# Heads' scores from high and low parts, softmax scaling on ScalarE and gate blocks of 384 columns in a decoder layer

## What is computed

```python
H_SB, H_MOBA, H_DSA, HEAD_DIM = 6, 5, 5, 64
def hybrid_mixer(h, w_in, b_gate, w_proj_sb, w_proj_moba, w_proj_dsa, w_o, slopes):
    proj = h @ w_in
    (q_sb, k_sb, v_sb, q_mb, k_mb, v_mb, q_ds, k_ds, v_ds,
     q_ix, k_ix, w_ix, gate_logits) = jnp.split(proj, _mixer_split_points(), axis=-1)
    o_sb = stick_breaking_attention(heads(q_sb), heads(k_sb), heads(v_sb))
    o_mb = moba_attention(heads(q_mb), heads(k_mb), heads(v_mb), slopes[0::2])
    o_ds = dsa_attention(heads(q_ds), heads(k_ds), heads(v_ds), q_ix..., k_ix, w_ix, slopes[1::2])
    g_sb, g_mb, g_ds = jnp.split(jax.nn.sigmoid(gate_logits + b_gate), N_BRANCH, axis=-1)
    merged = g_sb * (o_sb @ w_proj_sb) + g_mb * (o_mb @ w_proj_moba) + g_ds * (o_ds @ w_proj_dsa)
    return merged @ w_o
```

## Time and profile before

| | |
|---|---|
| median of 3 runs | 456.76 us (456.65 to 457.12) |
| the profiled execution | 456.9 us |
| its span, first to last instruction | 455.2 us |
| granted TensorE clock, mean | 0.996 |
| first projection units (0 to 9) | until about 56 us |
| units 10 to 50, with the heads | 56 to 213 us |
| merged heads and output projection | 213 to 261 us |
| SwiGLU | 261 to 455 us |

### The profile page before, as it was taken

How to read it: one execution, slowest core, us unless ns; L and a number is a source line. 1 busy time by engine, 2 the same in 40 slices (tenths; PEclk the granted TensorE clock), 3 DMA queues, 4 the chain that set the end, 5 groups by cost and what they waited for, 6 DMA issues and landing times.

```text
span 455.2 us, 7884 instructions
## 1 busy us (share of the span) xinstructions
PE 440.2 (97%) x2966; PEld 388.9 (85%) x2966; DVE 330.7 (73%) x587; ACT 243.6 (54%) x432; POOL 35.1 (8%) x76
## 2 busy tenths in 40 slices
PE   5999999999999999999999999999999999999994
PEld 3678998999999899999997899888888888888883
DVE  4625659887898887866995785896696687677655
ACT  4413885565777755587554676443534525425332
POOL 2000102100322231000000001000000000000000
PEclk9999999999999999999999999999999999999998
DMA  8999376797688558745559516998748658530002
GB/s 291 383 377 341 115 257 200 278 303 261 233 286 308 157 185 313 237 140 194 181 224 351 203 49 194 371 314 268 234 157 291 201 184 275 185 138 0 1 0 92
DMA packets 61634, 99.86 MB, mean 219 GB/s; under 512 B 3892, under 2 KB 44452, under 8 KB 61604
## 3 DMA queue, kind: packets, MB, share of 16 engines
q1 hardware_dynamic: 56480, 81.57, 52.8%
q0 software_dynamic: 4960, 17.84, 11.2%
q10 hardware_dynamic: 164, 0.05, 0.0%
HBM read 98.40 MB, written 1.05 MB: 218 GB/s over the span
## 4 chain that ended last, share of the span: by engine, by line
PE 91%; DVE 4%; issue 2%; ACT 2%; DMA 1%; SPq 0%; DVEq 0%; ACTq 0%
PE psum L1579 17%; PE psum L1982 16%; PE psum L1580 16%; PE psum L1581 16%; PE psum L1983 8%; PE psum L1641 3%; PE psum L1929 3%; PE psum L1595 2%; PE psum L1768 1%; DVE wlo L1113 1%; DMA xt<-in_x_dram 1%; PE psum L1703 1%; PE psum L1701 1%; PE psum L1630 1%; PE psum L1750 1%
## 5 line engine op out<-in xcount | busy, mean ns | idle before, releaser
L1982 PE MATMUL psum<-hcut,whi 128*128 128x512 f32 x320 | 111.5, 392 | 0.0
L1983 PE MATMUL psum<-hcut,wlo 128*128 128x256 f32 x320 | 89.5, 280 | 0.0
L1579 PE MATMUL psum<-hcut,whi 128*128 128x256 f32 x280 | 82.1, 293 | 0.3 <-DVE wlo L1113 0.3
L1580 PE MATMUL psum<-hcut,whi 128*128 128x256 f32 x280 | 79.1, 283 | 0.0
L1581 PE MATMUL psum<-hcut,wlo 128*128 128x256 f32 x280 | 79.1, 282 | 0.0
L1113 DVE TENSOR_TENSOR wlo<-raw,whi 128x768 fp32r<-128x768 f32 (+3 forms) x68 | 64.4, 972 | 15.6 <-ACT whi L749 15.0
L1982 PEld LDWEIGHTS psum<-hcut,whi 128*128 128x128 f32 x320 | 59.9, 187 | 13.2
L1983 PEld LDWEIGHTS psum<-hcut,wlo 128*128 128x128 f32 x320 | 60.4, 189 | 0.3
L749 ACT ACTIVATE whi<-raw 128x768 fp32r<-128x768 f32 (+3 forms) x68 | 55.6, 850 | 6.4 <-PE psum L1893 3.2
L1579 PEld LDWEIGHTS psum<-hcut,whi 128*128 128x128 f32 x280 | 53.4, 191 | 5.5 <-ACT qk L829 1.8
L1580 PEld LDWEIGHTS psum<-hcut,whi 128*128 128x128 f32 x280 | 53.5, 191 | 0.0
(11 more groups left out here) (252 smaller groups left out, 830.8 us busy)
## 6 DMA issues: line engine op xcount, KB each, us to landing
raw<-in_w_up_dram SPq DMA_DIRECT2D x22, 1024.0 KB, 7.5
xn<-in_w_ada_dram POOLq DMA_DIRECT2D x32, 512.0 KB, 4.9
raw<-in_w_in_dram SPq DMA_DIRECT2D x6, 2048.0 KB, 8.9
draw<-in_w_down_dram SPq DMA_DIRECT2D x11, 1024.0 KB, 5.0
ada<-in_w_ada_dram SPq DMA_DIRECT2D x16, 384.0 KB, 9.3
raw<-in_w_in_dram SPq DMA_DIRECT2D x3, 1536.0 KB, 8.9
raw<-in_w_o_dram SPq DMA_DIRECT2D x8, 512.0 KB, 4.5
raw<-in_w_in_dram SPq DMA_DIRECT2D x3, 1280.0 KB, 7.2
```

Source lines behind the costliest of these rows:

```text
L1579: pe.matmul(dst, a[0], b[0], start=first, stop=False)
L1580: pe.matmul(dst, a[0], b[1], start=False, stop=False)
L1982: pe.matmul(dst[:, :], wh, hcut[:, k, :, :].rearrange("p a s -> p (a s)"), start=k == 0, stop=False)
L1983: mm = pe.matmul(dst[:, S:2 * S], wl, hhi[:, k, :], start=False, stop=k == KC - 1)
```

## The change

Four things:

- **Parts for scores.** Of the 16 units with queries or keys of mb, sb and ds heads (`LOW_UNITS`) ScalarE writes the high part, in float32r, into `qk_hi`, and VectorE makes the low part (`take_low`), 20 instructions in all, into free columns of `whi` and `wlo` (`qk_low`). Scores are then `head_products`: three passes for each of the two column ranges, heads of a pair in turn. The indexer's logits stay float32.
- **New waits.** A new semaphore `unit_low`: TensorE's `unit(u)` waits for the low part of unit u-2 where it has one, since the bank is written again; the scores wait for theirs, and the first two logit pairs for those of units 5 to 9. In VectorE's order the low part of unit u-1 stands first in unit u.
- **Scaling.** The reciprocal stays on VectorE (`sum_inverse`), the two multiplications go to ScalarE, after its output copy of the same unit.
- **Blocks.** Gate blocks have 384 columns: 8 blocks of 3 units in place of 6 of 4. This leaves columns 3072 to 4095 of each `whi` and `wlo` free for the low parts. `PIECES_AT` follows: two, one and one piece over three units, and for the block after the last one three and one.

```diff
+GATE_COLS = 3 * P
+GATE_BLOCKS = 3 * D // GATE_COLS
-MIX_BLOCKS += [(O_GATE + BANK * i, BANK) for i in range(GATE_BLOCKS)]
+MIX_BLOCKS += [(O_GATE + GATE_COLS * i, GATE_COLS) for i in range(GATE_BLOCKS)]
...
+LOW_UNITS = [n for n, u in enumerate(UNITS) if u[1] in ("two heads", "last head") or u[1] == "features" and u[4] >= T_QMB]
...
+        def qk_low(tile):
+            i = LOW_SLOT[tile]
+            return (whi + wlo)[i // 4][:, KC * GATE_COLS + S * (i % 4):KC * GATE_COLS + S * (i % 4 + 1)]
...
+                elif u in LOW_UNITS:
+                    for tile, p0, s0, np, scale in qk_parts(u):
+                        ins = act.activation(qk_hi[p0:p0 + np, tile, :], src[s0:s0 + np, 0:S], ACT.Copy, scale=scale)
...
+                if u in NORM_AT and NORM_AT[u] in SOFT_NO:
+                    n = NORM_AT[u]
+                    act.wait_ge(sum_inverse, SOFT_NO[n] + 1)
+                    for t, (c0, c1) in enumerate(((0, P), (P, CAUSAL))):
+                        ins = act.activation(bufp[n % 2][:, c0:c1], bufp[n % 2][:, c0:c1], ACT.Copy, scale=ssum[:, n % 2, t:t + 1])
+                    ins.then_inc(p_ready, 1)
...
+            def take_low(u):
+
+                dve.wait_ge(unit_read, 2 * (u // 2) + 2 if u < FIRST_UNIT else u + 1)
+                src = unit_place(u)
+                for tile, p0, s0, np, scale in qk_parts(u):
+                    low, high = qk_low(tile)[p0:p0 + np, :], qk_hi[p0:p0 + np, tile, :].bitcast(F32)
+                    ins = dve.scalar_tensor_tensor(low, src[s0:s0 + np, 0:S], scale, high, ALU.mult, ALU.subtract)
+                ins.then_inc(unit_low, 1)
...
             for u in range(FIRST_UNIT, N_UNITS):
+                for m in [m for m in LOW_UNITS if m == u - 1 or u == FIRST_UNIT and m < u]:
+                    take_low(m)
...
-                    then(dve.reciprocal(ssum[:, n % 2, :], ssum[:, n % 2, :]))
-                    for t, (c0, c1) in enumerate(((0, P), (P, CAUSAL))):
-                        ins = dve.tensor_scalar(bufp[n % 2][:, c0:c1], bufp[n % 2][:, c0:c1], ssum[:, n % 2, t:t + 1], None, ALU.mult)
-                    ins.then_inc(p_ready, 1)
+                    dve.reciprocal(ssum[:, n % 2, :], ssum[:, n % 2, :]).then_inc(sum_inverse, 1)
...
                     pe.wait_ge(unit_read, u - 1)
+                    if u - 2 in LOW_UNITS:
+                        pe.wait_ge(unit_low, lows_until(u - 2))
...
+            def head_products(heads, cols, rows, fresh, done=None):
+
+                for i, (a, b) in enumerate(((0, 0), (0, 1), (1, 0))):
+                    for dst, left, right, p0 in heads:
+                        mm = pe.matmul(dst[:, cols], left[a][p0:p0 + HD, rows[0]], right[b][p0:p0 + HD, rows[1]], start=fresh and i == 0,
+                                       stop=i == 2, skip_group_check=True)
+                        if done is not None and i == 2:
+                            mm.then_inc(done, 1)
+
+            def query_major_cut(heads, done):
+
+                head_products(heads, slice(0, P), (slice(0, P), slice(0, P)), True)
+                head_products(heads, slice(P, CAUSAL), (slice(P, S), slice(0, S)), True, done)
```

More of the change, by code:

```diff
@@ L122, in mix_units @@
     for g in range(3 * D // P):
-        units.append((11 + g // 4, "gate", g % 4 * P, P, g))
+        units.append((11 + g * P // GATE_COLS, "gate", g * P % GATE_COLS, P, g))
     return units
@@ L129, with lows_until @@
 FIRST_GATE = N_UNITS - 3 * D // P
+LOW_UNITS = [n for n, u in enumerate(UNITS) if u[1] in ("two heads", "last head") or u[1] == "features" and u[4] >= T_QMB]
+LOW_TILES = [t + n for t in (T_QMB, T_KMB, T_QSB, T_KSB) for n in range(3)] + [T_QDS, T_QDS + 1, T_KDS, T_KDS + 1]
+LOW_SLOT = {t: i for i, t in enumerate(LOW_TILES)}
+LOW_SLOT.update({T_QDS + 2: LOW_SLOT[T_QMB], T_KDS + 2: LOW_SLOT[T_KMB]})
+def lows_until(u):
+    return sum(1 for n in LOW_UNITS if n <= u)
 UNITS_DONE = [max(n for n, u in enumerate(UNITS) if u[0] == b) + 1 for b in range(N_MIX)]
@@ L357, in decoder_layer @@
         gated_part.close()
+        qk_part = ExitStack()
+        sb("qk_pad", [P, TT * D], scope=qk_part)
+        qk_hi = sb("qk_hi", [P, 3 * KC, S], F32R, scope=qk_part)
+        qk_part.close()
         cut_part = ExitStack()
@@ L405, in decoder_layer @@
         unit_read = sem("unit_read")
+        unit_low, sum_inverse = sem("unit_low"), sem("sum_inverse")
         gemv = sem("gemv")
@@ L472, in front_cols, with unit_place, qk_parts @@
             return slice(0, Q_COLS) if front else slice(Q_COLS, CHUNK_COLS)
+        def qk_low(tile):
+            i = LOW_SLOT[tile]
+            return (whi + wlo)[i // 4][:, KC * GATE_COLS + S * (i % 4):KC * GATE_COLS + S * (i % 4 + 1)]
+        def unit_place(u):
+            return first_place(u) if u < FIRST_UNIT else bank[B_UNIT + u % 2]
+        def qk_parts(u):
+            b, what, c0, n, dest = UNITS[u]
+            if what == "two heads":
+                return [(tile, p0, HD * part, HD, SCALE / SLOPES[8] if tile == T_QMB + 2 else 1.0) for part, (tile, p0) in enumerate(dest)]
+            if what == "last head":
+                return [(tile, 0, HD * part, HD, SCALE / SLOPES[9] if tile == T_QDS + 2 else 1.0) for part, tile in enumerate(dest)]
+            scale = SCALE if T_QSB <= dest < T_KSB else 1.0
+            if T_QMB <= dest < T_KMB:
+                scale = qscale[0:n, dest - T_QMB:dest - T_QMB + 1]
+            elif T_QDS <= dest < T_KDS:
+                scale = qscale[0:n, 3 + dest - T_QDS:4 + dest - T_QDS]
+            return [(dest, 0, 0, n, scale)]
         def block_view(buf, b):
@@ L808, in take_unit @@
                     ins = act.activation(wixt[HD:n, :], src[HD:n, 0:S], ACT.Copy)
+                elif u in LOW_UNITS:
+                    for tile, p0, s0, np, scale in qk_parts(u):
+                        ins = act.activation(qk_hi[p0:p0 + np, tile, :], src[s0:s0 + np, 0:S], ACT.Copy, scale=scale)
                 elif what == "features":
[L810 to L823 removed]
+                    ins = act.activation(qk[0:n, dest, :], src[0:n, 0:S], ACT.Copy)
                 elif what == "values":
```

36 lines of the change are left out of this document (12 added, 24 removed).

## The result

| | before | changed |
|---|---|---|
| median | 456.59 us (11 runs) | 458.51 us (11 runs) |
| lowest and highest | 456.07, 457.19 us | 457.03, 460.62 us |
| ratio of the times | | 1.0042, 95% interval 1.0027 to 1.0058 |
| profiled execution, span | 456.9, 455.2 us | 457.93, 456.2 us |
| granted TensorE clock, mean | 0.996 | 0.997 |

The change makes the kernel 1.9 us slower, where no change was forecast. It also makes it less steady: its times spread over 3.6 us, those of before over 1.1 us. The profiled execution shows 1.0 us of the loss.

The account below looks back on a forecast made before the run. The prediction took TensorE's own queue (busy 97%) as the bound. Its terms summed as 456.9 + 0 + 0.1 - 0.5 + 0.3 = 456.8 us, 456.7 us for the median, with a range of 455.0 to 459.0.

Parts of the forecast that it names:

- The score steps: Nine TensorE steps making the scores: +0.01 us in six, -0.04 in three, in all 0, as weight loads become the bound.
- rival D: Score products go by columns, the parts loading faster than the trace rows say: -1.5 us, 455.2 us; chance 0.12.
- rival B: Score steps get longer, side-by-side running lost or loads not overlapping: +3.4 to +4.7 us; chance 0.08.
- VectorE's new work: 20 low parts add 7 to 8.5 us on VectorE, removed multiplications give back 5; total time +0.1, ends 0 and +0.5.
- The 0.1 us at unit 26: TensorE's start of unit 26 (119.09 us) waits slightly for unit 24's two low parts, done at 119.05 plus a semaphore.
- Unit 27: First gate unit: smaller pieces are there before TensorE asks, so its wait for the last piece goes; -0.5 us.
- Unit 36: Its gate block's last piece stands behind VectorE's longest stretch, the w_ada wait vanishing; +0.3 us, ends 0 and +1.7.
- Rival A: At unit 36 the w_ada wait stays and VectorE is late: stall 1.7 us instead of 0.3, 458.1 us; chance 0.16.
- ScalarE and transfers: ScalarE's added multiplications shift VectorE harmlessly, and gate block loads keep about 1 us of room; 0, upper end +2 us.
- Rival C: Low parts or blocks come late in several units, half a microsecond to 2 in all, 457.8 us as middle; chance 0.12.

Follow-up runs that it names:

- late-load run: The kernel before with one wait added on SP, so the second projection block's load goes out near 202.3 us, not 198.2: 457.04 us, ratio 1.0004.
- blocks only: The kernel before with gate blocks of 384 columns and nothing else: 457.92 against 456.88 us, ratio 1.0016.

## Why the prediction was wrong

Point by point, by its own steps:

- **The score steps: right.** 0.88 to 0.89 us query-major and 0.83 to 0.84 key-major (0.86 and 0.81 forecast), loads 0.11 apart, pairs side by side. Neither the rule of products by columns (rival D) nor lost overlap (rival B) came. By the rule of the Trainium skill that the prediction weighed (TensorE: Matmul & The Clock Gate, Part 3) a step would be 1.23 us; the trace disagrees here too. The runs agree with the forecast: all of the change without the passes is as slow as all of it.
- **VectorE's new work: right in kind.** The low parts took 0.41 to 0.48 us each. The 0.1 us at unit 26 didn't come: counted from the same start units 25 and 26 are both 0.08 late in the changed kernel, and that comes from the score steps before them, each query-major one 0.03 longer.
- **Unit 27: right.** -0.5 forecast, -0.53 to -0.55 in the profiles of the changed kernel.
- **Unit 36: the mechanism right, the term mis-sized.** +0.3 forecast, +0.61 to +0.62 measured. The wait for the part of `w_ada` did vanish. Counted from the same start TensorE asked at 159.72 (159.8 forecast) and the piece ended at 160.10 (160.05), so it was 0.4 late. But I counted only the lateness: the first product after a wait comes some 0.15 us later still and is 0.08 longer. That was in the earlier trace rows at unit 27, where I had counted it. Rival A (the wait stays) was wrong.
- **The step that failed is "ScalarE and transfers": "Loads of 1.5 MB take 8.9 us, which leaves about 1 us in the worst place. 0, upper end +2."** It looked only at gate blocks and their units. A buffer's next load hangs on the last piece of the block in it, and behind the last gate blocks stand the projection blocks. Two things made such pieces late: the blocks (for the second projection block the cut moves from unit 46 to 47 and the load from 198.2 to 201.3; for the third it starts 0.5 us later) and the scaling that stands ahead of them on ScalarE (to 202.5, and another 0.5 us for the third). Then the chunk of w_o, the third block and the gain rows run into each other, and the third block had 0.6 us to spare. Measured: 0.9 to 1.8 us in five profiles instead of 0. The text also said that the scaling shifts VectorE's pieces by up to 0.5 us where TensorE asks later, and asked what TensorE waits for, but not what SP waits for.
- Rival C ("Low parts or blocks come late in several units (slower), half a microsecond to 2 in all", 0.12) is nearest to what happened, though its blocks were not the ones that were late.

What stays open: how much of the loss is the third block's late start and how much its slower transfer. From the late-load run to blocks only it lands 1.9 us later from the same start: 0.6 of it is the start, 1.3 the transfer (10.2 and 11.6 us), with one profile each. The transfers issued behind the gain row may be a reason for the second part: with one of them the block took 9.8 to 10.2 us, with two 10.3 and 11.6, with three 9.9 to 11.9. The ranges overlap, and no run delayed the third block's load alone. Nor was it seen what the slowest runs, 460 us and more, do.

## What to carry to other kernels

Where a tile schedule is shortened or shifted, follow each buffer's release to the load that waits for it, past the end of the stage that is changed: the loads of the next stage hang on the last pieces of this one. Ask for each load which piece releases it: here the second block's and the third block's hung on pieces of two different blocks. Then look at the stage in which an engine has no idle time and a transfer lands with half a microsecond to spare; what comes later there costs all of its delay beyond that. Before a transfer is moved out of the way, look up when its data are read (441 us here, and it was loaded at 211) and what it will stand beside in its new place.

## What the runs showed of the hardware

The third projection block is 1152 KB in seven loads of SP. With neither gain row beside it, it took 6.0 to 6.6 us from the first issue to the last completion; with one gain row of 512 KB from GpSimd beside it 8.0 to 8.6 us; with both, 9.8 to 11.9 us. Each 512 KB on the other queue cost it about 2 us or more, and with both of them it also differed most from one execution to the next. The Trainium skill (DMA: Bandwidth & Descriptors, "Issuing engines are not separate DMA queues") says that all issuing engines use the same 16 DMA engines, which interleave their queues. By that rule a load from GpSimd is not free beside one from SP; the runs agree.

Not expected was how far such a microsecond travels. 1 MB moved from 211 to 237 us in the kernel before, in time for its own readers, made it 2.6 us slower, as ScalarE waited 3.7 us for the first SwiGLU weights.
